# Spreading 48 multiply-adds of the modulation rows unevenly over twelve convolution blocks, and moving the sums of the rows with them

## The reference, cut to what matters

```python
mod = jnp.einsum("bd,lde->lbe", jax.nn.silu(c), ada_w) + ada_b[:, None, :]
...
sh1, sc1, g1, sh2, sc2, g2 = jnp.split(mod[l][:, None, :], 6, axis=-1)
u = x * (1.0 + sc1) + sh1
...
bch = u @ w_in
b_gate, c_gate, h = jnp.split(bch, 3, axis=-1)
z = c_gate * h
z = lax.conv_general_dilated(z, conv_w[:, None, :], ...) + conv_b
return (b_gate * z) @ w_out
```

## Time and profile before

| | |
|---|---|
| median of 3 runs | 1482.23 us (1479.53 to 1485.29) |
| the profiled execution | 1481.74 us, its span 1479.9 us |
| mean granted TensorE clock | 0.926 |
| busy | TensorE 87%, VectorE 73%, ScalarE 52%, GpSimd 20% |

### The profile page before, as it was taken

The page is one execution under the profiler, slowest core; times in us unless marked ns, Lnnn a source line. Parts: engine busy times, 40 slices in busy tenths (PEclk is TensorE's granted clock), DMA queues, the critical chain, the costliest instruction groups (busy, mean ns, idle before and its releaser), DMA issues.

```text
span 1479.9 us, 18395 instructions
## 1 busy us (share of the span) xinstructions
PE 1292.0 (87%) x6603; PEld 1003.2 (68%) x6603; DVE 1081.8 (73%) x1201; ACT 770.4 (52%) x998; POOL 301.6 (20%) x344
## 2 busy tenths in 40 slices
PE   1399997849999999987989899999984999999985
PEld 0277765747777777746987677775783777777762
DVE  5648783768889888855884676665368898889867
ACT  0323221317777777754443555567142777777760
POOL 3011111410000000016101554545251100000020
PEclk9699998859999999997989899999976999999998
DMA  8657775319999999951711333330633999999972
GB/s 307 233 178 242 268 245 211 137 48 356 411 389 380 387 390 378 399 198 43 219 62 58 101 101 92 106 117 4 242 114 115 375 403 389 387 384 385 397 286 86
DMA packets 107568, 356.07 MB, mean 241 GB/s; under 512 B 8034, under 2 KB 16446, under 8 KB 107470
## 3 DMA queue, kind: packets, MB, share of 16 engines
q1 hardware_dynamic: 82984, 269.52, 48.6%
q0 software_dynamic: 19952, 69.83, 13.5%
q10 hardware_dynamic: 4566, 15.84, 2.6%
HBM read 330.99 MB, written 25.21 MB: 241 GB/s over the span
## 4 chain that ended last, share of the span: by engine, by line
PE 39%; issue 30%; DVE 15%; ACT 7%; DMA 5%; POOL 3%; ACTq 0%; DVEq 0%; POOLq 0%
PE bank L233 9%; PE bank L235 8%; PE bank L234 8%; DVE acc L361 3%; PE bank L1927 2%; PE bank L1909 2%; DMA xg<-scratch_u,tok 2%; POOL prob L2144 2%; ACT w_hi L1107 2%; PE bank L1897 1%; DMA ada<-in_ada_w_dram 1%; PE bank L894 1%; DVE xt L594 1%; ACT prob L2045 1%; POOL xg L1043 1%
## 5 line engine op out<-in xcount | busy, mean ns | idle before, releaser
L1113 DVE TENSOR_TENSOR w_lo<-raw,w_hi 128x2048 fp32r<-128x2048 f32 x189 | 436.9, 2316 | 69.5 <-ACT w_hi L1107 67.5
L1107 ACT ACTIVATE w_hi<-raw 128x2048 fp32r<-128x2048 f32 x189 | 362.5, 1919 | 84.9 <-PE bank L235 75.0
L233 PE MATMUL bank<-w_lo,xe_hi 128*128 128x512 f32 x512 | 211.9, 414 | 9.6 <-DVE xe_lo L1070 9.4
L235 PE MATMUL bank<-w_hi,xe_hi 128*128 128x512 f32 x512 | 203.8, 398 | 0.0
L234 PE MATMUL bank<-w_hi,xe_lo 128*128 128x512 f32 x512 | 203.6, 398 | 0.0
L228 DVE TENSOR_TENSOR w_lo<-raw,w_hi 128x2048 fp32r<-128x2048 f32 x37 | 85.5, 2316 | 114.2 <-ACT w_hi L223 114.0
L233 PE MATMUL bank<-u_lo,w_hi 128*128 128x512 f32 x320 | 133.7, 418 | 17.8 <-DVE q L1814 9.3
L1043 POOL DMA_INDIRECT xg<-scratch_u,tok x32 | 36.2, 1132 | 554.3 <-DVE tok L1037 553.7
L223 ACT ACTIVATE w_hi<-raw 128x2048 fp32r<-128x2048 f32 x37 | 70.5, 1910 | 139.0 <-PE bank L235 137.3
L234 PE MATMUL bank<-u_hi,w_lo 128*128 128x512 f32 x320 | 129.8, 406 | 0.0
L235 PE MATMUL bank<-u_hi,w_hi 128*128 128x512 f32 x320 | 129.8, 406 | 0.0
(11 more groups left out here) (289 smaller groups left out, 2357.6 us busy)
## 6 DMA issues: line engine op xcount, KB each, us to landing
raw<-in_w_gu_dram SPq DMA_DIRECT2D x128, 1024.0 KB, 7.7
raw<-in_w_down_dram SPq DMA_DIRECT2D x64, 1024.0 KB, 8.3
ada<-in_ada_w_dram POOLq DMA_DIRECT2D x64, 512.0 KB, 5.4
ada<-in_ada_w_dram SPq DMA_DIRECT2D x32, 512.0 KB, 3.8
scratch_y<-ye ACTq DMA_DIRECT2D x30, 512.0 KB, 7.5
raw<-in_conv_w_in_dram SPq DMA_DIRECT2D x12, 1024.0 KB, 11.8
raw<-in_w_kv_dram SPq DMA_DIRECT2D x6, 1024.0 KB, 8.5
rows<-scratch_mods POOLq DMA_DIRECT2D x10, 512.0 KB, 7.4
```

Of the source, the lines that this page charges most:

```text
L233: nc.tensor.matmul(o, lh, rl, start=start, stop=False)
L235: return nc.tensor.matmul(o, lh, rh, start=False, stop=stop)
L1107: nc.scalar.activation(w_hi[:, hslot, :], raw[:, slot, :], ACT.Copy).then_inc(hi_done, 1)
L1113: nc.vector.tensor_tensor(w_lo[:, slot, :], raw[:, slot, :], w_hi[:, hslot, :].bitcast(F32), ALU.subtract).then_inc(lo_done, 1)
```

## The change

The 48 multiply-adds are spread over the passes by a table: 6, 6, 6, 2, 6, 4, 6, 6, 5, 1, 0, 0. A second table gives the block ahead of which each row is summed: row 2 ahead of block 2, row 3 ahead of 3, row 4 ahead of 5, row 5 ahead of 8, row 6 ahead of 9, row 7 ahead of 11. The copies and the store on ScalarE take the same passes. Nothing is added or left out: the same 48 multiply-adds, six sums, six pairs of copies and stores, and the same transfers.

```diff
-        MACS_FIRST, MACS_SLOT = 16, 4
+        MACS_FIRST = 16
+        MACS = (6, 6, 6, 2, 6, 4, 6, 6, 5, 1, 0, 0)
+        SUM_AT = {2: 2, 3: 3, 5: 4, 8: 5, 9: 6, 11: 7}
...
         def conv_pe(pe):
             for b in range(N_CIN):
                 g, kh = b // 2, b % 2
-                if b >= 3 and b % 2 == 1:
-                    mod_sums(pe, ada_a, (b + 1) // 2, bank[4:6])
+                if b in SUM_AT:
+                    mod_sums(pe, ada_a, SUM_AT[b], bank[4:6])
                 pe.wait_ge(lo_done, b + 1)
...
                 mm.then_inc(blk_used, 1)
-            mod_sums(pe, ada_a, 7, bank[4:6])
...
                 split_hi(act, b + NSPLIT)
-                if b >= 3 and b % 2 == 1:
-                    mod_rows(act, ada_a, (b + 1) // 2, bank[4:6])
-                    mod_store(act, ada_a, (b + 1) // 2)
-            mod_rows(act, ada_a, 7, bank[4:6])
-            mod_store(act, ada_a, 7)
+                if b in SUM_AT:
+                    mod_rows(act, ada_a, SUM_AT[b], bank[4:6])
+                    mod_store(act, ada_a, SUM_AT[b])
...
                 split_lo(dve, b + NSPLIT)
-                ada_macs(dve, ada_a, MACS_FIRST + MACS_SLOT * b, MACS_SLOT)
+                ada_macs(dve, ada_a, MACS_FIRST + sum(MACS[:b]), MACS[b])
```

## The result

The changed kernel takes 1517.38 us (median of 4 runs, 1514.73 to 1520.86) against 1481.89; the ratio is 1.0233, interval 1.0216 to 1.0250, that is 34.5 us more, between 32.0 and 37.0 (the plain difference of the two medians is 35.5). The forecast was 32.1 more, 1514. The profiled execution is one of 1519.07 us.

The account below looks back on a forecast made before the run. TensorE, busy 87% and running its queue in order, was taken as the bound. Waits 31.3, clock 5.1 and 0.9, extra sum 1.8, small waits -0.9 make +38.2; minus 6.1 gives +32.1 us, 1514, range 1505 to 1522.

Parts of the forecast that it names:

- The three waits on multiply-adds: TensorE idles ahead of the sums before blocks 2, 3 and 5 until `acc`: 8.1, 9.8 and 10.3 us.
- The fourth wait: Before block 9, row 6's sum waits for ScalarE's copy of row 5, behind a split: 3.1 us.
- The clock behind the waits: Sums after idle run slow: 1.7 us for each of three long waits, 5.1; 0.9 behind the 3.1 us wait.
- One sum more ahead of block 11, small waits gone: Six sums for five ahead of block 11, +1.8 us; small waits on products and `acc` go, -0.9.
- What is given back: Output projection starts 8.2 us after block 11, pays 1.7 slow start: effective 9.9 against 16.0, -6.1 us.
- The rest of the kernel: Behind the output projection's start, engines and DMA queues hang on `blk_used` and move as one; nothing more given back.
- That no new wait comes: Rival for the input blocks: waits and clock terms vanish, -5.2 us, 1477; chance 0.03.
- that the clock holds: Rival: the waits come but no slow matmuls follow, +24 us, 1507; chance 0.06.
- That the ring falls behind: Rival: six multiply-adds a slot, 8.1 us tile landings and slower starts behind waits, +39 us, 1522; chance 0.08.
- The opposite-sided reading: Rival that the change does what it says, with no new wait: -5.2 us, 1477; chance 0.03.

Follow-up runs that it names:

- the run with the waits filled: Changed kernel plus 32, 40 and 42 extra matmuls, results unused, ahead of the sums before blocks 2, 3 and 5: 1513.19 us, ratio 1.0209.
- refitted counts: From the changed kernel with the sums put back to their places before the change: counts 6, 6, 5, 4, 3, 4, 4, 5, 5, 6, 0, 0; 1478.25 us, ratio 0.9962.
- The two tries at the end of the stretch: From refitted counts: `v_lo` ahead of block 14's split in pass 11, 1480.57 us; row 7's sum held until ScalarE has split block 14, 1481.10 us.
- two kernels with the same timeline in this stretch: Refitted counts, ratio 0.9962, and the same with row 7's sum held until ScalarE has split block 14, ratio 0.9986.

## Why the prediction came out right, step by step

- **The three waits on multiply-adds:** 8.1, 9.8 and 10.3 forecast, 8.13, 9.75 and 10.26 measured. Shown to be the places: with them put back the loss is gone, and moving one sum costs 6.4 us (row 2) or gives back 9.6 (row 4).
- **The fourth wait:** 3.1 and 3.10, released by `modrow`, and gone when the copy is moved.
- **The clock behind the waits** is the term that was mis-sized. I had 1.7 for each long wait, the length of one sum. The low level lasted beyond the sum into the block: the row at 106.49 starts a run of slow matmuls to 108.8, about 1.0 us more, and there were 0.2 and 0.6 behind the other two. Together 6.9 us for 5.1; the run with the waits filled puts it at 7.1. Behind the 3.10 us wait the sum took 1.88 us, so 0 where I had 0.9. In all 6.9 for 6.0: too little for the long waits and too much for the short one partly cancel, and that the sum of the clock terms is only 0.9 off is in part luck. The Trainium skill's rule (TensorE: Matmul & The Clock Gate, on HAM oscillation) agrees for the three long waits and for the projection. I had applied it to the wait of 3.10 us as well, and there it did not hold; which of the short waits it holds for stays open (last section).
- **One sum more ahead of block 11, small waits gone:** +1.8 and -0.9 as worked out. Block 11 ends at 256.88+0.23 = 257.1, 38.9 after before's 218.26; forecast 38.2. Block 2's place in the queue was reached 0.3 earlier in this execution (94.7 for 95.0), so the stretch itself grew by 39.2; the waits (31.24), 6.9, 1.8 and -0.9 make 39.0.
- **What is given back:** the projection starts 265.34-257.11 = 8.2 behind block 11, as forecast, and its slow start costs 1.8 us for 1.7. At the second block of the projection TensorE is 32.6 us later than in the trace of before; the forecast has 32.1.
- **The rest of the kernel** was to move as one. In the two profiled executions, matmuls paired in order, the distance grows from 32.6 to 37.4 us by the end, but the same distance, taken for other kernels of this study, drifts either way behind the stretch (from 32.3 to 28.5 with the copy first in pass 8). The growth is not a new wait: from the third block of the projection to the last matmul the same 5867 matmuls keep TensorE busy for 1103.9 us of 1208.3 before and 1108.5 of 1213.1 in the changed kernel, so nearly all of the 4.8 us is in matmuls that take longer. Why they do stays open. The interval of the ratio, 32.0 to 37.0, includes 32.6.
- **The rivals.** That no new wait comes was refuted by three rows; that the clock holds, by the 3.57 us sums. That the ring falls behind took 0.7 us here and shows only in kernels that don't stop, where I had not priced it. The opposite-sided reading, that such a change can gain, was not far: with the old places and refitted counts it does, by 5.6 us by the ratio and 2.2 by the span of the trace.
- **What I left out for my own experiments.** The short waits on products that they brought out cost the clock too, 1.6 us behind 2.06, 2.52 and 2.65 us of idle time and 2.7 behind 3.55; I had priced the waits alone.
- **A step that was true and incomplete.** I had found that a copy behind a split holds the next sum, for block 9, and did not apply it to the sum behind block 11 in my own experiments. The two tries at the end of the stretch failed for it.

## What to carry to other kernels

Before moving work between two queues, write for each hand-over which block's end lets the producer start: a count table with the right totals says nothing if the consumer stands ahead of the block beside which the producer runs. A wait removed from an in-order engine is worth what the next-latest input leaves; list all of them, copies on a third engine included. And a slack that long waits had covered, here VectorE's late products and the ring, is a new bound as soon as the waits go. Compare variants that differ by less than 0.3% on one chip: two kernels with the same timeline in this stretch had ratios 0.24% apart on two chips.

## What the runs showed of the hardware that was not expected

The length of a short idle time did not settle what the clock did behind it. In the changed kernel an idle time of 3.10 us between blocks left the clock at the upper level (sum 1.88 us, granted clock 1.00 from 219.6 to 223), and so it did in the two other kernels that have this wait. Idles of 3.10 us in the attention stage were followed by slow matmuls. That TensorE is less full there does not explain it, for between the full blocks of this stretch shorter idles were followed by slow matmuls too: 2.06 us (row 4 summed later), 2.52 (refitted counts) and 2.65 (new counts, old places), each with a block of 13.0 us behind it. Idles of 1.23, 1.40 and 1.61 us left the clock up. What decides between 2 and 3.1 us no run here shows.

Behind idles of 8 to 10 us the slow spell lasted 3.9 to 5.8 us from the first matmul, so such a wait costs between 1.8 and 2.7 us on top of its length. The table of windows of the changed kernel, the hole of the third wait, the matmuls behind its sum, and the stretch behind the short wait (length, PE busy, granted clock, DMA share, GB/s):

```profile
154.90:165.34 10.44, 0.18 (x1) 0.74 0.66 206
168.80:171.00 2.20, 2.20 (x8) 0.68 0.97 346
...
219.60:223.00 3.40, 3.39 (x11) 1.00 0.94 313
```
